# Second layer's projections in fp32r high and low parts, three products for each fp32 matmul, weights in units of 256 columns

## The chip, the cores and the metric

One NeuronCore of a Trainium2 chip runs the whole program. Its engines work side by side, each with its own instruction queue, and wait for one another by semaphores: TensorE (PE in the profile; PEld is its weight load), VectorE (DVE), ScalarE (ACT), GpSimd (POOL) and SyncE (SP), which issues the large transfers. The metric is the time of one execution on the device in microseconds (us); the median of three runs counts.

## The reference

Two layers, one after the other, on 256 tokens of width 1024, all in fp32. The first is a block with mLSTM, sparse attention and 32 experts; the change doesn't touch it. The second computes

```python
h = rms_norm(x, norm_g) * (1.0 + scale) + shift
proj = h @ w_in                      # 1024 x 10084
(q, k, v, z_att, q_idx, k_idx, w_idx, z_ssm, xbc, dt_raw, gate_logits) = split(proj)
o_att = sparse_attention(q, k, v, q_idx, k_idx, w_idx) * silu(z_att)
y_att = o_att @ w_branch_att         # 1024 x 1024
xbc = silu(causal_depthwise_conv(xbc))
y = ssd(...) + d_skip * xs           # state-space scan, 4 groups of 8 heads, 2 chunks of 128 tokens
y = rms_norm(y * silu(z_ssm)) ; y_ssm = y @ w_branch_ssm     # 2048 x 1024
merged = sigmoid(gate_att) * y_att + sigmoid(gate_ssm) * y_ssm
x = x + gate * (merged @ w_out)      # 1024 x 1024
```

## The kernel before, in words

Activations of the second layer lie transposed in SBUF: `hT` is 128 partitions x 8 k tiles x 256 tokens. Weights come in slabs of 1024 rows x 512 columns (2 MB, `SLABS2`), through a ring of five slots (`slots`: two in `ring_low`, three in `first_ring`, which is also the ring of the first layer's experts). `load_slab` (L248) is run by SP; it waits until the slab that lay in the slot has been used (`b_slab_used`). All products are plain fp32. The stages of the second layer, each a block with a barrier at its end:

- Stage one (from L1627): `tokens_by_columns` (L260) makes q, k, v and the indexer's columns of four slabs, 512 or 356 columns moving, tokens stationary. ACT issues nine small transfers and computes sin and cos; DVE copies the results (L1670, L1673).
- Attention (from L1728): PE has the eight slabs of `z_att` and `xbc` as filler, in halves (`half_slab`, L281, called by `give`), between the steps of the attention. Program order on each engine is written by hand: `give(2)`, the indexer's turns, `give(3)`, q and k turned, and so on. ACT's `take` (L1757) evacuates each half, azT by Silu (L1765), the convolution's taps (L1776); a half may begin when the one before the last has been taken. DVE normalises and rotates the indexer's keys, then takes the sums of squares of q and k (L1931), which ACT's square (L1784) and, in program order, the first `take(2)` stand behind; then the top-k and the softmax.
- State space (from L2031): eight pairs (chunk c, group g), c = 0 and 1 in turn. PE has 16 fillers of `z_ssm` and gates (`fill`, two per pair) and four of the attention branch. For each pair: POOL makes a mask `L_` (L2040), PE sums it (`prepare`, L2109 and L2112), DVE cuts it (L2205, `seg_ready`), ACT takes exp (L2068), DVE multiplies (L2213, `m_ready`), PE makes y (L2151), DVE adds, gates by zs and squares (L2221 to L2231). For c = 0 there is also `xd` (L2196), the state copy `st` (L2211) and two matmuls. After the last pair: the norm of y (L2237) and the gating of the four attention fillers (L2243).
- Closing: PE turns y (L2270), ACT scales it into `yT` (L2303), then the branch product (L2282, 256 matmuls), DVE merges (L2315, L2316), w_out (`columns_by_tokens`, L274, 128 matmuls), residual adds (L2319), turns (L2293), copies (L2323, L2307) and the store.

The fp32r type is used in one place of the first layer: the rows for the experts are picked by products of one-hot columns with a high part (`h2h`, an ACT copy to fp32r) and a low part (`h2l`, a DVE subtraction), L1144, 512 columns moving.

Of the kernel before, what the change touches and what calls it, by code (L numbers as in the profile page):

```python
# [23 lines left out]
P = 128  # L24
# [27 lines left out]
SLOTS, SLOTS2 = 5, 5  # L52
# [94 lines left out]
SLABS2 = [("w_in_2", 0, [(0, c, 512)]) for c in (P_Q, P_Q + 512, P_K)]  # L147
SLABS2 += [("w_in_2", 0, [(0, P_QI, 324), (324, P_DT, 32)])]
SLABS2 += [("w_in_2", 0, [(0, P_ZA + 512 * n, 512)]) for n in range(2)]
SLABS2 += [("w_in_2", 0, [(0, P_XBC + 512 * n, 512)]) for n in range(6)]  # L150
Z_G = [(P_ZS, P_G + D), (P_ZS + 512, P_G + D + 512), (P_ZS + 1024, P_G), (P_ZS + 1536, P_G + 512)]
for z, gate_at in Z_G:
    SLABS2 += [("w_in_2", 0, [(0, z, 512)]), ("w_in_2", 0, [(0, gate_at, 512)])]
SLABS2 += [("w_branch_att_2", 0, [(0, 512 * n, 512)]) for n in range(2)]
SLABS2 += [("w_branch_ssm_2", D * k, [(0, 512 * n, 512)]) for n in range(2) for k in range(2)]
SLABS2 += [("w_out_2", 0, [(0, 512 * n, 512)]) for n in range(2)]
M_ZA, M_XBC, M_ZS, M_ATT, M_SSM, M_OUT = 4, 6, 12, 20, 22, 26
# [29 lines left out]
def two_layers(nc, A, cst_in, c32_in, out):  # L187
    with ExitStack() as ctx:
# [67 lines left out]

        def slab_count(specs, n):
            return 16 * sum(len(specs[m][2]) for m in range(n % len(slots), n + 1, len(slots)))

        def tokens_by_columns(pe, n, w, bank):  # L260

            for t in range(TT):
                for k in range(KT):
                    mm = pe.matmul(ps[:, bank + t, 0:w], hT[:, k, t * P:(t + 1) * P], slots[n % len(slots)][:, k, 0:w],  # L264
                                   start=(k == 0), stop=(k == KT - 1))
            return mm
# [1055 lines left out]
        with nc.Block() as block:  # L1322
# [5 lines left out]
            def _(sp):  # L1328
# [26 lines left out]
                for n in range(2):  # L1355
                    load_slab(sp, n, SLABS2[n], "b_")
                sp.wait_ge(s("", "down_used"), NE * DOWNS)
                for t in range(TT):
                    sp.wait_ge(s("", f"got0{t}"), 16)
                for n in range(2, SLOTS2):  # L1360
                    load_slab(sp, n, SLABS2[n], "b_")
# [247 lines left out]

        NH = QH + KVH
# [12 lines left out]
        if True:  # L1626
            with nc.Block() as block:  # L1627
                @block.sync
                def _(sp):
                    for n in range(SLOTS2, SLOTS2 + M_ZA):  # L1630
                        load_slab(sp, n, SLABS2[n], "b_")

                @block.scalar
                def _(act):
# [3 lines left out]
                    with nc.allow_non_contiguous_dma("256 positions"):  # L1638
                        act.dma_start(pos[:], A["positions_2"].rearrange("(t p) a -> p (t a)", p=P)).then_inc(sm("pos_in"), 16)
                    act.wait_ge(sm("angle_ready"), 1)  # L1640
                    S.link(act, act.activation(sin[:], ang[:], ACT.Sin))
                    S.done(act, act.activation(cos[:], ang[:], ACT.Sin, scale=0.5), sm("half_sin_ready"))
                    act.wait_ge(sm("bc_in"), 16 * len(BC))

                @block.tensor
                def _(pe):
                    for n in range(M_ZA):
                        pe.wait_ge(sm(f"b_slab_ready{n % len(slots)}"), slab_count(SLABS2, n))
                        tokens_by_columns(pe, n, 356 if n == 3 else 512, 2 * n).then_inc(sm("b_slab_used"), 1)

                @block.vector
                def _(dve):
                    dve.wait_ge(sm("pos_in"), 16)
# [12 lines left out]
                    for n in range(M_ZA):  # L1666
                        bank = 2 * n
                        dve.wait_ge(sm("b_slab_used"), n + 1)
# [9 lines left out]
        with ExitStack() as pi:  # L1678
# [14 lines left out]
            A1 = sb("A1", [P, QH, SEQ], at=pi)  # L1693
# [8 lines left out]
            HALVES = 2 * (M_ZS - M_ZA)  # L1702
            ZHALVES = 2 * (M_XBC - M_ZA)

            def half_made(eng, h):
                if h % 2:
# [653 lines left out]
```

## Time and profile before

| | us |
|---|---|
| median of three runs (1886.74 to 1889.82) | 1887.21 |
| the profiled execution | 1889.87 |
| its span, first to last instruction | 1888.1 |
| first layer | 0 to 1380 |
| stage one | 1380 to 1436, PE busy 54.0 |
| attention | 1436 to 1588, PE busy 136.7 |
| state space, up to the last pair | 1588 to 1753, PE busy 157.6 |
| attention branch and norm of y | 1753 to 1782, PE busy 27.7 |
| turning y | 1782 to 1791, PE busy 4.5 |
| branch product | 1791 to 1851, PE busy 57.5 |
| w_out, adds, turns, store | 1851 to 1888, PE busy 29.9 |

Mean granted TensorE clock 0.974 of full speed. Over the whole span DVE is busy 444.1 us, ACT 329.6, POOL 109.0; 545 MB are moved, most of them experts' weights of the first layer. In the rows below each line of a view is a group of instructions: engine, line of the kernel, operation, tile written <- tiles read, shape, count; a bracket gives the idle time of the engine just before, and what ended it.

### The profile page before, as it was taken

Reading aid. Unit: us, or ns where it says so; the run is one execution under the profiler, and the core shown is the slowest. Engines: PE = TensorE matmul, PEld = TensorE weight load, DVE = VectorE, ACT = ScalarE, POOL = GpSimd, SP = SyncE. Lnnn points to the kernel's source line nnn. Section 1 sums busy time; section 2 is a strip of 40 time slices with the busy share of each in tenths; the row PEclk is TensorE's granted clock in tenths of the full one; section 3 lists DMA queues with packets and bytes.
Section 4 is the critical chain, followed back from the end, with each engine's and each line's share of the span. In section 5 each row is a group of like instructions: output and inputs, shape, how many; then the busy total and the mean of one; then the engine's idle time right before and its main releaser. Section 6 shows DMA issues by size and latency. Waiting matters only on the chain. (4 is left out here: it accounts for less than half of the span.)

```text
span 1888.1 us, 37646 instructions
## 1 busy us (share of the span) xinstructions
PE 1779.0 (94%) x16403; PEld 979.4 (52%) x16403; DVE 444.1 (24%) x701; ACT 329.6 (17%) x643; POOL 109.0 (6%) x121
## 2 busy tenths in 40 slices
PE   6999988999999999999999999999679996999897
PEld 4875642443434343443434343444436885667786
DVE  2272171111101011111101011111325243334201
ACT  2334151000000000000000000000111374122200
POOL 0111020000000000000000000000000242110000
PEclk9999999999999999999999999999789998999999
DMA  9976385999999999999999999996834232223310
GB/s 342 351 281 228 130 332 229 388 405 406 387 405 391 408 393 402 393 403 394 406 396 396 401 395 403 395 401 275 320 119 149 95 132 86 90 90 134 134 45 23
DMA packets 150270, 545.33 MB, mean 289 GB/s; under 512 B 14712, under 2 KB 25224, under 8 KB 117352
## 3 DMA queue, kind: packets, MB, share of 16 engines
q1 hardware_dynamic: 134832, 519.48, 71.5%
q10 hardware_dynamic: 10968, 15.40, 2.2%
q0 software_dynamic: 4416, 9.69, 1.5%
q8 instruction: 37, 0.61, 0.1%
q14 instruction: 17, 0.14, 0.0%
HBM read 526.06 MB, written 17.84 MB: 288 GB/s over the span
## 5 line engine op out<-in xcount | busy, mean ns | idle before, releaser
L1397 PE MATMUL ps<-ring_low,xg 128*32 128x512 f32 x3072 | 343.8, 596 | 0.0
L1397 PE MATMUL ps<-first_ring,xg 128*32 128x512 f32 x3072 | 335.4, 592 | 0.0
L1397 PEld LDWEIGHTS ps<-first_ring,xg 128*32 128x32 f32 x3072 | 99.5, 110 | 230.1 <-issue 230.1
L1397 PEld LDWEIGHTS ps<-ring_low,xg 128*32 128x32 f32 x3072 | 96.4, 110 | 205.8 <-issue 200.0
L1528 DVE TENSOR_SCALAR gl<-ps 128x768 f32<-128x768 f32 x32 | 30.6, 958 | 683.2 <-PE ps L1397 683.2
L1420 PE MATMUL ps<-first_ring,aT 128*32 128x256 f32 x3072 | 173.3, 382 | 2.3 <-ACT aT L1479 2.3
L1420 PE MATMUL ps<-raw_more,aT 128*32 128x256 f32 x3072 | 171.7, 379 | 0.0
L285 PE MATMUL ps<-hT,first_ring 128*128 128x256 f32 x704 | 158.1, 385 | 3.3 <-ACT hT L478 1.8
L285 PEld LDWEIGHTS ps<-hT,first_ring 128*128 128x128 f32 x704 | 134.7, 193 | 25.2 <-issue 4.9
L1420 PEld LDWEIGHTS ps<-first_ring,aT 128*32 128x32 f32 x3072 | 100.4, 111 | 82.5 <-issue 20.2
L1420 PEld LDWEIGHTS ps<-raw_more,aT 128*32 128x32 f32 x3072 | 101.8, 110 | 64.1
L1473 ACT ACTIVATE sg<-gl 128x768 f32<-128x768 f32 x32 | 27.0, 845 | 511.6 <-DVE gl L1528 511.6
L1478 ACT ACTIVATE aT<-ps 128x576 f32<-128x576 f32 x32 | 20.9, 652 | 443.8 <-PE ps L1408 434.0
L285 PE MATMUL ps<-hT,ring_low 128*128 128x256 f32 x384 | 88.9, 394 | 3.2 <-ACT azT L1765 3.0
L285 PEld LDWEIGHTS ps<-hT,ring_low 128*128 128x128 f32 x384 | 75.9, 199 | 14.5 <-issue 3.6
L1539 DVE COPY ye<-ps 128x768 f32<-128x768 f32 x32 | 30.6, 958 | 212.1 <-PE ps L1420 212.1
L1367 POOL DMA_INDIRECT got<-y_dram,dest x8 | 7.6, 954 | 1075.6 <-DMA y_dram<-ye 1074.4
L1741 POOL TENSOR_TENSOR xbc<-xbc,taps 128x512 f32<-128x512 f32 x36 | 46.1, 1279 | 102.3 <-ACT xbc L1776 100.4
L2282 PE MATMUL ps<-xbc,first_ring 128*128 128x256 f32 x192 | 44.3, 393 | 3.4 <-ACT xbc L2303 3.4
L2282 PEld LDWEIGHTS ps<-xbc,first_ring 128*128 128x128 f32 x192 | 37.9, 198 | 9.2 <-ACT xbc L2303 3.6
L2126 PE MATMUL ps<-first_ring,hT 128*128 128x512 f32 x96 | 42.3, 593 | 0.0
L264 PE MATMUL ps<-ring_low,hT 128*128 128x512 f32 x64 | 30.3, 637 | 9.8 <-PEq L203 9.8
(474 smaller groups left out, 1555.4 us busy)
## 6 DMA issues: line engine op xcount, KB each, us to landing
first_ring<-in_w_up_dram SPq DMA_DIRECT2D x128, 1024.0 KB, 6.8
ring_low<-in_w_up_dram SPq DMA_DIRECT2D x128, 1024.0 KB, 7.0
raw_more<-in_w_down_dram SPq DMA_DIRECT2D x64, 1024.0 KB, 7.0
first_ring<-in_w_down_dram SPq DMA_DIRECT2D x64, 1024.0 KB, 7.1
first_ring<-in_w_in_dram SPq DMA_DIRECT2D x15, 2048.0 KB, 8.1
ring_low<-in_w_in_dram SPq DMA_DIRECT2D x9, 2048.0 KB, 8.2
first_ring<-in_w_ada_dram SPq DMA_DIRECT2D x7, 2048.0 KB, 20.3
ring_low<-in_w_ada_dram SPq DMA_DIRECT2D x5, 2048.0 KB, 18.0
```

Of the source, the lines that this page charges most:

```text
L264: mm = pe.matmul(ps[:, bank + t, 0:w], hT[:, k, t * P:(t + 1) * P], slots[n % len(slots)][:, k, 0:w], start=(k == 0), stop=(k == KT - 1))
L285: mm = pe.matmul(ps[:, bank, (j % 2) * SEQ:(j % 2 + 1) * SEQ], slots[n % len(slots)][:, k, j * P:(j + 1) * P], src[:, k, :], start=(k == 0 ...
L1367: pool.indirect_dma_start(got[:, t, BUFFER[j], :], None, y_dram[0:TOTAL, :], bass.IndirectOffsetOnAxis(dest[:, t, j:j + 1], 0))\
L1397: mm = pe.matmul(ps[32 * q:32 * q + 32, u, :], xg[:, k, 32 * block_of:32 * block_of + 32], w[:, :, 256 * f:256 * f + 256], start=False, st ...
L1420: mm = pe.matmul(ps[32 * q:32 * q + 32, 5 + u, 0:256], aT[:, f, 32 * block_of:32 * block_of + 32], w[:, 256 * part:256 * part + 256], star ...
L1473: act.activation(sg[:], gl[:], ACT.Sigmoid, scale=ALPHA).then_inc(s(tag, "sig_ready"), 1)
L1478: act.activation(aT[:, 0:6, :], flat[:, :, 0:ROWS], ACT.Copy).then_inc(s(tag, "aT_ready"), 1)
L1528: dve.tensor_scalar(gl[:], ps[:, 0:3, 0:256], LIMIT, None, ALU.min).then_inc(s(tag, "glu_ready"), 1)
L1539: dve.tensor_copy(ye[:], ps[:, 5:8, 0:256]).then_inc(s(tag, "ye_copied"), 1)
L1741: ins = pool.tensor_tensor(c, c, taps[:, i % 2, tap], ALU.add)
L2126: mm = pe.matmul(ps[:, 4 + f % 2, :], hT[:, k, (f % 2) * P:(f % 2 + 1) * P], slots[n % len(slots)][:, k, :], start=(k == 0), stop=(k == KT ...
L2282: mm = pe.matmul(ps[:, 2 * i + j // 2, (j % 2) * SEQ:(j % 2 + 1) * SEQ], slots[(n + k // KT) % len(slots)][:, k % KT, j * P:(j + 1) * P], ...
```

## The change

The slabs of the second layer become 56 units of 256 columns (1 MB each; the eight of `w_branch_ssm` are 2048 rows x 128 columns). They pass through three slots of 8 KB per partition in `ring_low`; its fourth quarter is reused as a scratch tile, and `first_ring` is given back after the first layer. Units 0 and 1 (first half of q) and the twelve units of the convolution stay plain fp32. The other 42 are split on chip: ACT copies the unit into an fp32r tile (`high`), DVE subtracts that from the unit into a second one (`low`), three stages of each. The moving side (`hT`, later `azT`, y and the merged tile) is split in the same way into `inh`, `inl`, `yh` and `yl`. Each split unit is three products: high x high, high x low, low x high. In the state-space stage z_ssm's fillers are 256 columns for both token tiles, so that both fillers of a pair are awaited before the gating. In the closing stage the split of the merged tile follows in quarters, the residual adds and turns follow k tile by k tile, and the output is stored in four parts.

```diff
+PLAIN = {0, 1} | set(range(U_XBC, U_ZS))
+SPLIT = {u: s for s, u in enumerate(u for u in range(len(UNITS2)) if u not in PLAIN)}
+RAWS, STAGES = 3, 3
...
+        def load_unit(sp, u):
+            if u >= RAWS:
+                if u - RAWS in SPLIT:
+                    sp.wait_ge(sm("u_low"), SPLIT[u - RAWS] + 1)
+                else:
+                    sp.wait_ge(sm("u_used"), u - RAWS + 1)
...
+        def make_high(act, u):
...
+            unit_there(act, u)
+            if s_ >= STAGES:
+                act.wait_ge(sm("u_used"), SPLIT_UNIT[s_ - STAGES] + 1)
+            act.activation(high[:, s_ % STAGES], raw2[u % RAWS], ACT.Copy).then_inc(sm("u_high"), 1)
+
+        def make_low(dve, u):
...
+            dve.wait_ge(sm("u_high"), s_ + 1)
+            dve.tensor_tensor(low[:, s_ % STAGES], raw2[u % RAWS], high[:, s_ % STAGES].bitcast(F32), ALU.subtract)\
+                .then_inc(sm("u_low"), 1)
...
+        def terms(u, src, srcs):
+            if u not in SPLIT:
+                return [(raw2[u % RAWS], src)]
+            hi, lo = high[:, SPLIT[u] % STAGES], low[:, SPLIT[u] % STAGES]
+            return [(hi, srcs[0]), (hi, srcs[1]), (lo, srcs[0])]
...
+        def unit_by_columns(pe, u, bank, src, srcs, groups=(range(KT),), come=None):
+            unit_ready(pe, u)
+            for j in range(2):
+                todo = [(g, a, x, k) for g in range(len(groups)) for a, x in terms(u, src, srcs) for k in groups[g]]
...
+                    mm = pe.matmul(ps[:, bank, j * SEQ:(j + 1) * SEQ], a[:, k, j * P:(j + 1) * P], x[:, k, :],
+                                   start=(i == 0), stop=(i == len(todo) - 1))
+            mm.then_inc(sm("u_used"), 1)
```

Stage one and attention:

```diff
                 def _(act):
...
+                    S.done(act, act.activation(inh[:], hT[:], ACT.Copy), sm("in_high"))
+                    make_high(act, 2)
                     act.wait_ge(sm("angle_ready"), 1)
...
+                    for u in range(3, U_ZA + 2):
+                        make_high(act, u)
...
                 def _(pe):
-                    for n in range(M_ZA):
...
+                    for u in range(U_ZA):
+                        n, c = divmod(u, 2)
+                        if u == 2:
+                            pe.wait_ge(sm("in_low"), 1)
+                        unit_by_tokens(pe, u, lambda t: ps[:, 2 * n + t, 256 * c:256 * c + unit_width(u)])
...
                     V.link(dve, dve.tensor_scalar(wix[:], idt[:, :, 320:324], IH ** -0.5 * ID ** -0.5, None, ALU.mult))
+                    make_low(dve, U_ZA + 2)
                     dve.wait_ge(sm("dev_ready"), 1)
...
+                    make_low(dve, U_ZA + 3)
                     for t in range(TT):
                         dve.wait_ge(sm("head_sq"), t + 1)
```

State space and closing:

```diff
                         S.done(act, act.activation(M[:, i % 2], M[:, i % 2], ACT.Exp), sm("seg_exp"))
                         for f in (2 * i, 2 * i + 1):
+                            make_high(act, U_ZS + f + 2)
                             fill_made(act, f)
...
+                        if f == 16:
+                            pe.wait_ge(sm("in_high"), 2)
+                            pe.wait_ge(sm("in_low"), 2)
...
                                                       ALU.min), sm("seg_ready"))
+                        make_low(dve, U_ZS + 2 * i + 2)
                         if c == 0:
                             dve.wait_ge(sm("st_made"), g + 1)
...
+                        make_low(dve, U_ZS + 2 * i + 3)
+                        if i == len(PAIRS) - 1:
+                            dve.wait_ge(sm("in_high"), 2)
+                            V.done(dve, dve.tensor_tensor(inl[:], azT[:], inh[:].bitcast(F32), ALU.subtract), sm("in_low"))
                         dve.wait_ge(sm("y_made"), i + 1)
...
+                    pe.wait_ge(sm("yh_ready"), 16)
+                    pe.wait_ge(sm("yl_ready"), 16)
...
+                    for c in range(4):
+                        unit_by_columns(pe, U_OUT + c, c, None, (inh, inl), (range(6), range(6, 8)), None if c else come)
+                    for k in range(KT):
+                        pe.wait_ge(sm("x3_ready"), k + 1)
```

## Rows read from the trace of the kernel before

**Rows 1.** The page: span, and PE's busy time, share and instructions.

```profile
span 1888.1 us, 37646 instructions
...
PE 1779.0 (94%) x16403; PEld 979.4 (52%) x16403; DVE 444.1 (24%) x701; ACT 329.6 (17%) x643; POOL 109.0 (6%) x121
```

**Rows 2.** Stretches: busy us (instructions) of PE, PEld, DVE, ACT, POOL; clock, DMA share, GB/s.

```profile
1453.00:1460.00 7.00, 6.71 (x23) 5.66 (x24) 6.62 (x12) 1.73 (x4) 0.00 (x0) 0.76 0.54 207
...
1607.00:1753.00 146.00, 146.00 (x659) 104.95 (x659) 58.54 (x77) 37.26 (x39) 15.94 (x7) 1.00 0.29 102
...
1791.00:1851.00 60.00, 57.50 (x256) 49.88 (x256) 4.81 (x4) 0.00 (x0) 0.00 (x0) 0.96 0.10 35
```

**Rows 3.** Groups of PE from 1380 us on: busy us, mean ns.

```profile
L285 PE MATMUL ps<-azT,ring_low 128*128 128x256 f32 x128 | 27.8, 379 | 0.0
...
L2126 PE MATMUL ps<-ring_low,hT 128*128 128x512 f32 x32 | 14.1, 594 | 0.0
```

**Rows 4.** PE's timeline at L1144 (start, us), and the load's ns (tile h2h).

```profile
270.76 0.39 PE L1144 MATMUL ps<-hot,h2l 128*128 128x512 f32 x1
...
273.03 0.39 PE L1144 MATMUL ps<-hot,h2l 128*128 128x512 f32 x1
...
L1144 PEld LDWEIGHTS ps<-hot,h2h x32: 186/188/188, 267.5 to 285.1; 128*128 128x128 f32 x32
```

**Rows 5.** PE's timeline: start us, us of the whole group, count.

```profile
1615.47 1.95 PE L2112 MATMUL ps<-cst,xbc 128*128 128x128 f32 x16
1617.25 7.03 PE L2126 MATMUL ps<-first_ring,hT 128*128 128x512 f32 x16
...
1624.98 1.89 PE L2151 MATMUL ps<-y,xbc 128*128 128x64 f32 x16
```

**Rows 6.** Single lines over 2048 elements: ns min/median/max.

```profile
L1793 ACT ACTIVATE qT<-ps x1: 1877/1877/1877, 1479.1 to 1479.1; 128x2048 f32<-128x2048 f32 x1
...
L2185 DVE TENSOR_TENSOR y<-xs,dts x2: 2291/2997/3703, 1597.5 to 1601.2; 128x2048 f32<-128x2048 f32 x2
...
L2237 DVE TENSOR_TENSOR y<-y,gs x2: 2291/2292/2293, 1759.6 to 1761.9; 128x2048 f32<-128x2048 f32 x2
```

**Rows 7.** DMA issues: count, KB each, median us to landing.

```profile
first_ring<-in_w_in_dram SPq DMA_DIRECT2D x15, 2048.0 KB, 8.1
...
first_ring<-in_w_in_dram SPq DMA_DIRECT2D x1, 1296.0 KB, 11.4
```

**Rows 8.** Timeline at the start of the second layer.

```profile
1386.09 1.28 ACT L1641 ACT_TABLE_LOAD   x1 [8.67 <-issue]
...
1397.07 1.23 DVE L1670 COPY qkv<-ps 128x1024 f32<-128x1024 f32 x1 [4.24 <-PE ps L264]
```

**Rows 9.** Timeline at the start of the attention stage.

```profile
1452.55 1.23 ACT L1765 ACTIVATE azT<-ps 128x512 f32<-128x512 f32 x2
...
1453.29 22.64 PE L285 MATMUL ps<-hT,ring_low 128*128 128x256 f32 x96 [3.03 <-ACT azT L1765]
```

**Rows 10.** Timeline of one pair in the state-space stage.

```profile
1626.98 0.69 DVE L2223 COPY y<-ps 128x512 f32<-128x512 f32 x1 [9.52 <-PE ps L2151]
...
1631.66 1.22 DVE L2205 TENSOR_TENSOR xbc<-ps,cst 128x1024 f32<-128x1024 f32 x1
1632.96 1.28 ACT L2068 ACT_TABLE_LOAD   x1 [7.98 <-DVE xbc L2205]
```

**Rows 11.** PE's timeline: the attention branch.

```profile
1752.88 27.85 PE L285 MATMUL ps<-azT,ring_low 128*128 128x256 f32 x128
```

**Rows 12.** Timeline of the closing stage: PE's waits, adds and turns.

```profile
1790.83 33.49 PE L2282 MATMUL ps<-xbc,first_ring 128*128 128x256 f32 x144 [3.40 <-ACT xbc L2303]
...
1851.14 14.08 PE L274 MATMUL ps<-mer,ring_low 128*128 128x256 f32 x64 [2.64 <-DVE mer L2316]
...
1879.14 2.04 DVE L2319 SCALAR_TENSOR_TENSOR xT<-ps,mod,xT 128x256 f32<-128x256 f32 x4 [11.76 <-PE ps L274]
...
1881.24 1.97 PE L2293 MATMUL ps<-cst,xT 128*128 128x128 f32 x16 [2.21 <-DVE xT L2319]
```

More of the change, by code:

```diff
@@ L50 @@
 XBC = DI + 2 * SG * SN
-SLOTS, SLOTS2 = 5, 5
+SLOTS = 5
 RV = 3 * P - 1
@@ L146, with halves @@
     0, 1024, 1280, 1536, 2560, 2816, 2880, 2884, 4932, 8004, 8036)
[L147 to L150, printed above, removed]
+def halves(name, row, c0):
+    return [(name, row, [(0, c0 + 256 * c, 256)]) for c in range(2)]
 Z_G = [(P_ZS, P_G + D), (P_ZS + 512, P_G + D + 512), (P_ZS + 1024, P_G), (P_ZS + 1536, P_G + 512)]
[L152 to L157, printed above, removed]
+UNITS2 = sum((halves("w_in_2", 0, c) for c in (P_Q, P_Q + 512, P_K)), [])
+UNITS2 += [("w_in_2", 0, [(0, P_QI, 256)]), ("w_in_2", 0, [(0, P_QI + 256, 68), (68, P_DT, 32)])]
+U_ZA = len(UNITS2)
+UNITS2 += halves("w_in_2", 0, P_ZA) + halves("w_in_2", 0, P_ZA + 512)
+U_XBC = len(UNITS2)
+UNITS2 += sum((halves("w_in_2", 0, P_XBC + 512 * n) for n in range(6)), [])
+U_ZS = len(UNITS2)
+UNITS2 += sum((halves("w_in_2", 0, c) for pair in Z_G for c in pair), [])
+U_ATT = len(UNITS2)
+UNITS2 += halves("w_branch_att_2", 0, 0) + halves("w_branch_att_2", 0, 512)
+U_SSM = len(UNITS2)
+UNITS2 += [("w_branch_ssm_2", 0, [(0, P * c, P)]) for c in range(KT)]
+U_OUT = len(UNITS2)
+UNITS2 += halves("w_out_2", 0, 0) + halves("w_out_2", 0, 512)
+PLAIN = {0, 1} | set(range(U_XBC, U_ZS))
+SPLIT = {u: s for s, u in enumerate(u for u in range(len(UNITS2)) if u not in PLAIN)}
+SPLIT_UNIT = list(SPLIT)
+RAWS, STAGES = 3, 3
 BC = {"q_norm_g_2": (0, HD), "k_norm_g_2": (HD, HD), "idx_k_ln_g_2": (2 * HD, ID), "idx_k_ln_b_2": (2 * HD + ID, ID),
@@ L1354, in _ @@
                 sp.wait_ge(s("", "up_used"), NE * UPS)
[L1355 to L1361, printed above, removed]
+                for u in range(RAWS):
+                    load_unit(sp, u)
             @block.gpsimd
@@ new lines, in terms, with unit_by_tokens @@
+        def terms(u, src, srcs):
+            if u not in SPLIT:
+                return [(raw2[u % RAWS], src)]
+            hi, lo = high[:, SPLIT[u] % STAGES], low[:, SPLIT[u] % STAGES]
+            return [(hi, srcs[0]), (hi, srcs[1]), (lo, srcs[0])]
+        def unit_by_tokens(pe, u, bank_of):
+            unit_ready(pe, u)
+            w = unit_width(u)
+            todo = [(a, x, k) for a, x in terms(u, hT, (inh, inl)) for k in range(KT)]
+            for t in range(TT):
+                for i, (a, x, k) in enumerate(todo):
+                    mm = pe.matmul(bank_of(t), x[:, k, t * P:(t + 1) * P], a[:, k, 0:w], start=(i == 0),
+                                   stop=(i == len(todo) - 1))
+            mm.then_inc(sm("u_used"), 1)
@@ L2079, in _ @@
                                 S.done(act, act.activation(dst, src, ACT.Sigmoid), sm("fill_taken"))
+                    S.done(act, act.activation(inh[:], azT[:], ACT.Copy), sm("in_high"))
+                    make_high(act, U_ATT + 2)
                     act.wait_ge(sm("gs_ready"), 1)
                     S.done(act, act.activation(gs[:], gs[:], ACT.Sqrt), sm("gs_rms"))
+                    for u in range(U_ATT + 3, U_SSM + 2):
+                        make_high(act, u)
                 @block.tensor
@@ new lines, in _ @@
+                    pe.wait_ge(sm("yl_ready"), 16)
+                    for c in range(KT):
+                        u = U_SSM + c
+                        unit_ready(pe, u)
+                        todo = [(as_tall(a), x, k) for a, x in terms(u, None, (yh, yl)) for k in range(2 * KT)]
+                        for i, (a, x, k) in enumerate(todo):
+                            mm = pe.matmul(ps[:, 4 + c // 2, (c % 2) * SEQ:(c % 2 + 1) * SEQ], a[:, k, :], x[:, k, :],
+                                           start=(i == 0), stop=(i == len(todo) - 1))
+                        mm.then_inc(sm("u_used"), 1)
@@ new lines, in _ @@
+                    for m in range(4):
+                        if m == 0:
+                            make_high(act, U_SSM + 2)
+                            make_high(act, U_SSM + 3)
+                        for u in (U_SSM + 2 * m + 4, U_SSM + 2 * m + 5):
+                            if u < U_OUT + 2:
+                                make_high(act, u)
+                        act.wait_ge(sm("mer_ready"), m + 1)
+                        S.done(act, act.activation(tile2(inh, m), tile2(mer, m), ACT.Copy), sm("mh_ready"))
```

225 lines of the change are left out of this document (131 added, 94 removed).

## The prediction, made before the changed kernel was run

> **What bounds the kernel now.** I read the page first: PE, the matmul engine, is busy 94% of a span of 1888.1 us [rows 1]. The busy time by stage then shows where the second layer (from 1380 us on) stands: PE is busy for all but a little of the state-space stage (from 1607) and of the closing one (from 1791), while VectorE (DVE) has 58.5 of 146 us and 4.8 of 60, and the DMA share is 0.29 and 0.10 [rows 2]. So the layer is bound by matmul instructions, with free time on DVE, ScalarE (ACT) and the DMA rings, except at a few joints where PE waits for a chain of DVE and ACT work [rows 9, 12]. After such a wait the granted clock can fall to its half, 1.2 GHz: it is 0.76 over 1453 to 1460, behind a wait of 3.0 us [rows 2, 9], so some 3.4 of the 7 us ran at half speed, which costs 1.7.
>
> The sum is made against the profiled execution, 1889.9 us, of which 1888.1 are the span; it lies 2.7 us above the median of the runs shown (1887.2), so I take 2.7 off at the end.
>
> **Price of a product.** A plain fp32 matmul with 256 moving columns is two instructions: 128 of them are busy for 27.8 us, so 0.216 us a step, 0.432 us per matmul [rows 3]. A unit (1024 x 256 weights against 256 tokens) is 16 such matmuls: 6.9 us. The split unit has 48 fp32r products in place of the 16. The trace holds fp32r products only with 512 columns: ten steps from 270.76 to 273.03, so 0.227 us each, one instruction and not two [rows 4]. A 512-column fp32 instruction steps at (7.03 - 0.59)/15 = 0.429 [rows 3, 5], which is two passes of 0.214; the fp32r one is thus one pass plus 13 ns. With 256 columns a pass is 0.107. But each product has its own weight load. The bound from below is the load: fp32 instructions with 64 and with 128 columns both step at 0.108 to 0.112 us ((1.89 - 0.275)/15 and (1.95 - 0.275)/15), so the load of 128 columns sets that pace [rows 5]. The fp32r load is recorded at 187 ns, the fp32 load at 190 in the same place, so I take them as equal. The bound from above is that nothing of the recorded 187 ns overlaps [rows 4]. I take 0.122: the load's pace plus most of the 13 ns; the 128-column row, with load and pass equally long, is the nearest. A split unit is then 48 x 0.122 = 5.9 us against 6.9, 1.0 us less; below 0.144 it gains.
>
> The Trainium skill (TensorE: Matmul & The Clock Gate, Step-by-step) says that loading the next tile's weights takes no read bandwidth from the running matmul. By it the 13 ns would not come from the load, the step would stay at 0.112 and each unit would be 5.4 us; the fp32r row has the 13 ns, and I go by the row.
>
> **Price of the splits.** 42 of the 56 units are split: an ACT copy over 2048 elements, 1.88 us, and a DVE subtraction, 2.29 us, 3.0 on average where GpSimd works beside it [rows 6]. That is 79 us on ACT and 96 us on DVE in 508 us. It is free only where the chain that PE waits for doesn't contain it.
>
> **Loads.** 1 MB in place of 2 MB per transfer, three slots in place of five. 2 MB land in 8.1 us; a transfer of 1296 KB in narrower rows took 11.4 us while others ran [rows 7]. I take 4 to 8 us per unit: less than the 17 us in which three units are used. A split unit's slot is free after its subtraction, long before PE is done. I cost them at nothing; behind them stands only the start.
>
> **Stage one, eight units (1380.4 to 1434.0).** Units 0 and 1 are plain and end where the first copy of results starts now, 16.6 us in [rows 8]. Unit 2 needs hT copied and subtracted and itself split. ACT is issuing transfers until 1386 [rows 8]; 2 x 1.88 + 2 x 2.29 behind it gives 1393, before 1397. Unit 3 loads from 1390 on and is split by 1400, in time. Five units of 5.9 and the narrow one (48 x 0.112 = 5.4) give 34.7: end at 51.3 us instead of 53.6. **-2.3.**
>
> **Attention stage.** Two subtractions now stand ahead of DVE's sums of squares, which the ACT evacuation at 1452.6 waits for, and PE waits for that until 1453.3 [rows 9]. 2 x 2.29 = +4.6 before PE goes on; PE's wait grows from 3.0 to about 8 us and the low clock behind it lasts longer (+1.7). Against this two split units (-2.1) give **+4.2.** The twelve convolution units are unchanged; the splits of the first two gate units lie where DVE waits for PE.
>
> **State-space stage.** Now a pair of head groups takes PE 19.2 or 17.6 us in turn; with four units of 5.9 for two pairs PE would need 17.2 and 15.6. The chain is nearly as long. On DVE: tail of the pair before and decay mask, 5.9 us from 1626.98 to the end of the instruction at 1631.66 (6.6 where `xd` comes first) [rows 10]; then ACT's table load and exp, 2.4; then ACT's copy, 1.9, which is queued ahead of DVE's first subtraction, 2.3; then the state copy (0.7, every other pair), the mask product 1.25, `t5` 0.7 or none, the second subtraction 2.3. The sums are 17.0 and 17.7 us. So DVE sets the pace behind the first pair, and the eight save 7.9 us, not 16. The last pair also waits for the split of azT: ACT copy behind the last evacuation, subtraction to 19.3 us after the pair's start; PE idles 3.7 us and likely runs at half clock for a while (+1.7, as above). Then DVE has the tail, three subtractions and the scaling (4.6) before it gates the first attention unit, at 34 us; PE waits for it once more. The four units end 46.0 us after the pair's start instead of 43.6 (16.0 + 27.6) [rows 11]: +2.4. Together **-5.5.**
>
> **Closing stage.** Turning y takes 1.0 us longer (last subtraction behind ACT's last copy): +1.0. Eight units of branch weights: 46.9 us, and 2.2 for the slow clock after the wait of 3.4, against 57.7: -8.6. The splits keep one unit ahead. The wait before w_out, 2.6 us now, is about 1.9 as only the last two k tiles are late: -0.7. Four units of 5.9 against 27.8: -4.4. From the last w_out product to the end 9.0 us now (1879.1 to 1888.1): four adds 2.0, sixteen turns 2.0, the copies, the store. The adds and turns of six of eight tiles move under the last units, and copies and stores go in halves: about 1.0 + 0.6 + 0.7 + 3.7 = 6.0, -3.0 [rows 1, 12]. **-15.7.**
>
> Sum: -2.3 + 4.2 - 5.5 - 15.7 = -19.3, so 1870.6 for the profiled execution and **1868 us** for the median.
>
> **Rivals.**
> - The step is 0.112, the floor set by the load [rows 5]. The stages where PE sets the pace hold some 21 split units, about 1000 products, so each ns is 1.0 us: 10 us less, 1858. For it: the plain rows. Against: the fp32r row. Chance 0.15.
> - The splits are late. In the state-space stage each subtraction that meets GpSimd's mask costs up to 1.4 us (3.7 against 2.29 behind the mean of 3.0 in rows 6); 8 pairs give 11 us, 1879. For it: both stand in the same pair. Against: the mask is made while DVE waits for exp. Chance 0.14.
> - The other side: the load of an fp32r product doesn't hide under a pass as short as itself. Place: every split unit; it decides from a step of 0.141 on. At 0.187, the recorded load, the 21 units cost 65 us more and the others, once PE is behind in them too, about 50: 1980. For it: no row has a fp32r pass shorter than twice its load [rows 4]. Against: fp32 with a pass of equal or half length steps at the load's pace [rows 5]. Chance 0.12, most of it between 1884 and 1980. The Trainium skill (same page, The mechanism) has the rule that a weight load overlaps running matmuls only when its row group differs. All loads here use all rows, so load and pass would follow one another: 0.112 + 0.107 = 0.219 us, three products 0.66, some 2040 us. By that rule the 64-column row would step at about 0.16; it steps at 0.108 to 0.112, so I give it 0.02 of the 0.12.
> - The change doesn't do what it says: the products are lowered to two instructions again. The fp32r type is used so already and gives one [rows 4]. Chance 0.01, far slower.
>
> **How the numbers follow.** The forecast, -8 to -30 us with the step between 0.117 and 0.133, has 0.58. Low end: 1852, the floor of the step and a state-space stage without the two waits. High end: 1886, the late splits and a step of 0.128 together. Left out: nearly all of the slow rival and a little below. A measurement of this kernel can tell 0.2%, 3.8 us, from no change. Faster by more: 0.58 + 0.15 + most of 0.14 = 0.79 less a little for the joints; within: 0.08; slower 0.14.
>
> **What would show it.** Right: fp32r instructions of 256 columns, 48 per unit, stepping at 0.12; PE in the closing units 47 us; PE waits of 1 to 2 us per pair in the state-space stage, released by DVE; one wait of some 8 us in place of the 3.0 in the attention stage; DVE subtractions of 2.3 us; the tail 6 us. Wrong: a step off 0.12 moves the whole sum at 1 us per ns; waits of PE for loads would mean the slots are too few; DVE subtractions over 3 us would be the late splits.

## The result, and the profile of the changed kernel

The changed kernel takes 1862.85 us (median of 4 runs, 1861.0 to 1865.6), the kernel before 1887.68 in the same comparison: a ratio of 0.987, 95% interval [0.9857, 0.9881]. That is 24.8 us less; the forecast was 19.3 less, 1868. The profiled execution took 1861.18 us, its span is 1859.4. It lies 1.7 us below its median, and the one of before 2.2 above (1889.87), so the spans, which the table below compares, differ by 28.7.

The page of the changed kernel, the same two lines as in [rows 1]:

```profile
span 1859.4 us, 39736 instructions
...
PE 1740.1 (94%) x17331; PEld 1017.3 (55%) x17331; DVE 555.9 (30%) x770; ACT 415.5 (22%) x692; POOL 106.4 (6%) x121
```

PE has 928 more instructions and is busy for 38.9 us less. DVE and ACT have 112 and 86 us more, as the splits were costed (96 and 79, with the copies of the inputs on top). PE's share stays close to 94%. Of the 38.9 us of busy time that PE saved, 28.7 are out of the span, about three quarters; the other 10.2 have become idle time of PE.

Where the 28.7 us between the two spans (1888.1 and 1859.4) went, from PE's timelines. A stretch runs to the start of the same work in both kernels; only the eight pairs end with PE's last product of `y`, and the wait behind it counts with the attention branch:

| stretch | before | after | difference | forecast |
|---|---|---|---|---|
| up to the second layer's first product | 1380.4 | 1378.9 | -1.5 | 0 |
| stage one, eight units | 55.1 | 52.7 | -2.5 | -2.3 |
| attention stage | 152.5 | 152.5 | 0.0 | +4.2 |
| turning x, first decay products | 19.5 | 19.3 | -0.2 | 0 |
| eight pairs | 145.4 | 136.2 | -9.2 | -7.9 |
| attention branch with its waits | 29.2 | 30.9 | +1.7 | +2.4 |
| turning y | 8.8 | 10.1 | +1.3 | +1.0 |
| branch product and the wait behind it | 60.3 | 48.5 | -11.8 | -9.3 |
| w_out, then to the end | 37.0 | 30.4 | -6.6 | -7.4 |

**The product.** PE's timeline in stage one (start us, us of the group, count), where plain and split units meet:

```profile
1390.79 5.13 PE L1686 MATMUL ps<-ring_low,hT 128*128 128x256 f32 x23
1395.56 1.30 PE L1686 MATMUL ps<-high,inh 128*128 128x256 f32 x8
...
1398.62 1.12 PE L1686 MATMUL ps<-high,inh 128*128 128x256 f32 x8
1399.58 1.12 PE L1686 MATMUL ps<-high,inl 128*128 128x256 f32 x8
1400.54 1.12 PE L1686 MATMUL ps<-low,inh 128*128 128x256 f32 x8
...
1428.05 1.06 PE L1686 MATMUL ps<-high,inl 128*128 128x100 f32 x8
1428.95 1.06 PE L1686 MATMUL ps<-low,inh 128*128 128x100 f32 x8
```

Eight products start every 0.96 us: the step is 0.120 us, where 0.122 was taken from [rows 4, 5]. A split unit is 48 x 0.120 = 5.76 us against 6.9. The last unit, 100 columns wide, steps at 0.112 (eight in 0.90 us).

**The attention joint.** The timeline that answers to [rows 9]. DVE's subtraction of a weight unit (L1662) stands ahead of the sums of squares, ACT's evacuation waits for these, and PE for the evacuation:

```profile
1444.10 2.29 DVE L1662 TENSOR_TENSOR low<-ring_low,high 128x2048 fp32r<-128x2048 f32 x1
...
1446.31 1.48 DVE L2029 TENSOR_REDUCE ssum<-sq 128x10 f32<-128x1280 f32 x1
...
1452.72 1.23 ACT L1861 ACTIVATE azT<-ps 128x512 f32<-128x512 f32 x2
...
1453.37 2.08 PE L1698 MATMUL ps<-inh,high 128*128 128x256 f32 x8 [7.85 <-ACT azT L1861]
```

**A pair in the state-space stage.** DVE's timeline that answers to [rows 10], from the decay mask (L2306) to the end of the mask product (L2315):

```profile
1625.30 1.22 DVE L2306 TENSOR_TENSOR xbc<-ps,cst 128x1024 f32<-128x1024 f32 x1
1631.00 2.29 DVE L1662 TENSOR_TENSOR low<-ring_low,high 128x2048 fp32r<-128x2048 f32 x1 [4.48 <-ACT high L1655]
1633.21 1.22 DVE L2315 TENSOR_TENSOR xbc<-xbc,cb 128x1024 f32<-128x1024 f32 x1
```

and ACT's between them:

```profile
1626.60 1.28 ACT L2165 ACT_TABLE_LOAD   x1 [7.97 <-DVE xbc L2306]
1627.89 1.06 ACT L2165 ACTIVATE xbc<-xbc 128x1024 f32<-128x1024 f32 x1
1628.98 1.92 ACT L1655 ACTIVATE high<-ring_low 128x2048 fp32r<-128x2048 f32 x1
```

The reader is to see a loop: mask, table load, exp, copy, subtraction, mask product. The exp is done at 1628.95, but the mask product starts 4.3 us later: DVE first waits for ACT's copy (1.9) and then subtracts (2.3). Two pairs take 34.26 us (1626.90 to 1661.16), 17.49 and 16.77 in turn, against 17.7 and 17.0 in the forecast. PE's idle time in it is small, since it was given work to the brim: single waits of 0.2 to 0.5 us, some 1.0 us in two pairs, and 2.5 before the last `y`:

```profile
1626.58 0.49 PE L2213 MATMUL ps<-xbc 128*128 128x128 f32 x2 [0.19 <-DVE xbc L2306]
1626.90 1.95 PE L2216 MATMUL ps<-cst,xbc 128*128 128x128 f32 x16
...
1644.39 1.95 PE L2216 MATMUL ps<-cst,xbc 128*128 128x128 f32 x16
...
1661.16 1.95 PE L2216 MATMUL ps<-cst,xbc 128*128 128x128 f32 x16
...
1737.54 2.00 PE L2252 MATMUL ps<-y,xbc 128*128 128x64 f32 x16 [2.48 <-DVE xbc L2315]
```

**The closing stage**, PE's timeline (answers to [rows 11, 12]): the attention branch starts after a wait and loses time to the lower clock; the first unit of the branch product starts at the lower clock as well; behind that sixteen products start every 1.88 us.

```profile
1742.95 2.05 PE L1698 MATMUL ps<-inh,high 128*128 128x256 f32 x8 [3.41 <-issue]
1744.80 1.91 PE L1698 MATMUL ps<-inl,high 128*128 128x256 f32 x8
...
1757.36 1.21 PE L1698 MATMUL ps<-inh,high 128*128 128x256 f32 x8 [1.03 <-DVE ring_low L2353]
...
1780.54 3.54 PE L2394 MATMUL ps<-yh,high 128*128 128x256 f32 x16 [3.54 <-issue]
1783.88 2.20 PE L2394 MATMUL ps<-yl,high 128*128 128x256 f32 x16
...
1823.46 2.04 PE L2394 MATMUL ps<-yl,high 128*128 128x256 f32 x16
1825.34 2.04 PE L2394 MATMUL ps<-yh,low 128*128 128x256 f32 x16
1829.03 0.95 PE L1698 MATMUL ps<-inh,high 128*128 128x256 f32 x6 [1.65 <-DVE inl L2455]
...
1852.87 1.91 PE L2406 MATMUL ps<-cst,xT 128*128 128x128 f32 x16
```

**Splits and loads.** The page's groups of the two halves of a split, and its DMA issues (KB each, median us to landing; answers to [rows 6, 7]):

```profile
L1662 DVE TENSOR_TENSOR low<-ring_low,high 128x2048 fp32r<-128x2048 f32 x42 | 98.7, 2350 | 121.5 <-ACT high L1655 121.0
L1655 ACT ACTIVATE high<-ring_low 128x2048 fp32r<-128x2048 f32 x42 | 80.4, 1915 | 65.8 <-PE ps L2394 20.5 <-PE ps L1698 16.5 <-DMA ring_low<-in_w_in_dram 11.5
...
ring_low<-in_w_in_dram SPq DMA_DIRECT2D x39, 1024.0 KB, 5.3
```

A subtraction is 2.35 us on average: 40 of the 42 took 2.29, and two took 3.13 and 3.88, both at a time when GpSimd was at work as well. ACT waits 11.5 us in all for loads, and PE for none of them.

### The profile page after: what moved, and what is told of

It is laid out like the page before. It is cut to its first block and busy times, and to the rows that moved or that the text cites. A ratio compares the mean times of both kernels' runs of the same rounds, so it can differ in the third digit from the quotient of the medians.

```text
span 1859.4 us, 39736 instructions
## 1 busy us (share of the span) xinstructions
PE 1740.1 (94%) x17331; PEld 1017.3 (55%) x17331; DVE 555.9 (30%) x770; ACT 415.5 (22%) x692; POOL 106.4 (6%) x121
## 5 line engine op out<-in xcount | busy, mean ns | idle before, releaser
L1662 DVE TENSOR_TENSOR low<-ring_low,high 128x2048 fp32r<-128x2048 f32 x42 | 98.7, 2350 | 121.5 <-ACT high L1655 121.0
L1655 ACT ACTIVATE high<-ring_low 128x2048 fp32r<-128x2048 f32 x42 | 80.4, 1915 | 65.8 <-PE ps L2394 20.5
L1698 PE MATMUL ps<-inh,high 128*128 128x256 f32 x320 | 49.0, 293 | 16.1 <-ACT azT L1861 7.8
L321 PE MATMUL ps<-hT,first_ring 128*128 128x256 f32 x256 | 58.7, 389 | 1.8 <-ACT hT L514 1.8
L321 PEld LDWEIGHTS ps<-hT,first_ring 128*128 128x128 f32 x256 | 49.2, 194 | 11.5 <-issue 4.7
L1698 PEld LDWEIGHTS ps<-inh,high 128*128 128x128 f32 x320 | 43.2, 198 | 17.1 <-ACT azT L1861 8.1
```

The lines of the kernel that those rows point to most:

```text
L321: mm = pe.matmul(ps[:, bank, (j % 2) * SEQ:(j % 2 + 1) * SEQ], slots[n % len(slots)][:, k, j * P:(j + 1) * P], src[:, k, :], start=(k == 0 ...
L1655: act.activation(high[:, s_ % STAGES], raw2[u % RAWS], ACT.Copy).then_inc(sm("u_high"), 1)
L1662: dve.tensor_tensor(low[:, s_ % STAGES], raw2[u % RAWS], high[:, s_ % STAGES].bitcast(F32), ALU.subtract)\
L1698: mm = pe.matmul(ps[:, bank, j * SEQ:(j + 1) * SEQ], a[:, k, j * P:(j + 1) * P], x[:, k, :], start=(i == 0), stop=(i == len(todo) - 1))
```

## The experiments

Theory A at the start: the fp32r price of the three products is the whole gain, and in the stages where DVE or ACT is in PE's chain the splits decide what arrives. The rivals: the gain is that of the new order, the smaller units and the reordered tail; or PE sets the pace in the pairs too.

**All units plain.** The order, the units of 256 columns and the tail stay; no weight unit is split, and the products are plain fp32. The copies of the inputs and their low parts are still made, though no product reads a low part, and PE still waits for them.

```diff
-PLAIN = {0, 1} | set(range(U_XBC, U_ZS))
+FIRST_PLAIN = {0, 1} | set(range(U_XBC, U_ZS))
+PLAIN = set(range(len(UNITS2)))
...
-        inh = sb("inh", [P, KT, SEQ], F32R)
+        inh = sb("inh", [P, KT, SEQ])
...
-                return [(raw2[u % RAWS], src)]
+                return [(raw2[u % RAWS], src if u in FIRST_PLAIN else srcs[0])]
```

> The changed kernel with its units, its order and its closing tail, but all 56 units in plain fp32 against a plain copy of the activations. No output changes. Theory A (the gain is the price of three fp32r products, 48 steps of 0.120 us a unit against 32 of 0.216, and the new tail and the shorter first stage give some 5 us at most): each of the 42 units costs 1.15 us more where PE sets the pace; in the state-space stage DVE loses its 16 subtractions, so the pairs go to PE's 19.2 and 17.6 us; together 1880 to 1886 us, close to the kernel before. Theory B (the new order, the smaller units and the tail made the gain, and the products are about even): 1860 to 1868.

Measured: 1890.8 us against 1887.6 for the kernel before, ratio 1.0013 [1.0004, 1.0023]. A unit is back at 32 instructions of 0.216 us:

```profile
1612.89 7.07 PE L1687 MATMUL ps<-ring_low,inh 128*128 128x256 f32 x32
...
1752.52 22.67 PE L1699 MATMUL ps<-inh,ring_low 128*128 128x256 f32 x92 [3.56 <-DVE inl L2325]
```

So the order, the smaller units and the tail, with the splits of the inputs still in, together bring nothing; the whole of the 28 us between this run and the changed kernel is the fp32r products with their weight splits. A's number was 1880 to 1886, some 5 us too low. The tail gives what was expected: from the first branch product to the end it is 92.4 us in place of 97.3. But PE waits 3.56 us before the attention branch, where the kernel before has no wait [rows 11], and turning `y` takes 1.3 us more, and both waits are for low parts that this kernel doesn't need (`inl`, `yl`). Without them it might be some 5 us faster (an estimate from these two waits; no such kernel was run), so this run doesn't show that order and tail by themselves are worth nothing.

**The third product left out.** Low part of the weights times high part of the input is not computed.

```diff
-            return [(hi, srcs[0]), (hi, srcs[1]), (lo, srcs[0])]
+            return [(hi, srcs[0]), (hi, srcs[1])]
```

> In the changed kernel the third product (low x high) of every split unit is left out, everything else stays, splits too: 16 products of 0.120 us fewer a unit. Theory A (PE sets the pace in stage one, at the first two attention units and in the closing stage, DVE and ACT in the state-space pairs): up to 1.9 us for each of some 20 units, little in the pairs (0 to 2 us in all) and 2 to 4 in the attention branch; together 30 to 40 us less, 1823 to 1833, and the state-space pairs stay at 16.5 to 17.1 us. Theory B (PE sets the pace everywhere): 42 x 1.9 = 80 us less, 1783.

Measured: 1832.2 us, ratio 0.9707 [0.9689, 0.9725], theory A's number. PE's timeline over two pairs:

```profile
1614.70 1.95 PE L2216 MATMUL ps<-cst,xbc 128*128 128x128 f32 x16
...
1622.28 2.51 PE L2252 MATMUL ps<-y,xbc 128*128 128x64 f32 x16 [1.81 <-DVE xbc L2315]
...
1648.63 0.49 PE L2213 MATMUL ps<-xbc 128*128 128x128 f32 x2 [2.26 <-DVE xbc L2306]
1648.95 1.28 PE L2216 MATMUL ps<-cst,xbc 128*128 128x128 f32 x10
```

From 1614.70 to 1648.95 are 34.25 us for two pairs, with a third of the products of their four units gone; it is 34.26 with them. With less work for PE a pair gets no shorter. The chain through DVE and ACT sets it.

**A thin subtraction in the pairs.** The subtractions of the sixteen units in the pairs cover 32 elements of 2048; the rest of the low part is left out.

```diff
-            dve.tensor_tensor(low[:, s_ % STAGES], raw2[u % RAWS], high[:, s_ % STAGES].bitcast(F32), ALU.subtract)\
+            part = (slice(None), 0, slice(0, 32)) if U_ZS + 2 <= u < U_ATT + 2 else (slice(None),) * 3
+            dve.tensor_tensor(low[:, s_ % STAGES][part], raw2[u % RAWS][part], high[:, s_ % STAGES].bitcast(F32)[part],
+                              ALU.subtract)\
```

> In the changed kernel the DVE subtractions of the 16 units split inside the state-space pairs cover 32 elements a partition instead of 2048 (the low part of these units is otherwise left as it was, so part of the low x high product is wrong). Theory A (DVE's chain with ACT's copy and its two subtractions sets the pace of the pairs, 17.05 us on average measured): the pairs fall to what PE needs, about 16.1, so 7 us less, and 2 to 3 more after the last pair: 1852 to 1856. Theory B (PE and the exp set the pace, the subtractions are hidden): 1861 to 1864.

Measured: 1859.6 us, ratio 0.9853 [0.9833, 0.9873], between the two theories. The interval overlaps that of the changed kernel, so what the edit did is read from the trace, together with the next run's.

**ScalarE's copy moved.** In the pairs the copy of a unit stands behind the evacuation of the unit before it, no longer between the exp and DVE's first subtraction. Nothing is left out.

```diff
+                    make_high(act, U_ZS + 2)
                     for i, (c, g) in enumerate(PAIRS):
...
-                            make_high(act, U_ZS + f + 2)
...
+                            if f < 15:
+                                make_high(act, U_ZS + f + 3)
```

> The changed kernel with ACT's copy of each unit in the state-space pairs moved ahead of the wait for the decay mask and its exp, to behind the evacuation of the unit before. Nothing is left out. Theory A (DVE waits 4.5 us in each pair for exp and copy in a row; with the copy done early its subtraction runs beside exp, the DVE chain falls to about 13 us and PE sets the pace at 16.1): 7 to 8 us less, 1854 to 1857. Theory B (the copy only moves onto another critical place, the evacuations or the exp): 1861 to 1865, or slower.

Measured: 1857.7 us, ratio 0.9842 [0.9824, 0.9861], 0.7 above theory A's range and 3 below B's. DVE's timeline of the same pair as above: the subtraction now runs beside the exp, and the mask product starts 2.2 us after the mask's end instead of 6.7:

```profile
1628.39 1.23 DVE L2308 TENSOR_TENSOR xbc<-ps,cst 128x1024 f32<-128x1024 f32 x1
1629.65 2.29 DVE L1662 TENSOR_TENSOR low<-ring_low,high 128x2048 fp32r<-128x2048 f32 x1
1631.86 1.22 DVE L2317 TENSOR_TENSOR xbc<-xbc,cb 128x1024 f32<-128x1024 f32 x1
```

and PE's, over two pairs, with a single wait of 0.20 us:

```profile
1629.99 1.95 PE L2218 MATMUL ps<-cst,xbc 128*128 128x128 f32 x16
...
1662.76 0.49 PE L2215 MATMUL ps<-xbc 128*128 128x128 f32 x2 [0.20 <-DVE xbc L2308]
1663.08 1.95 PE L2218 MATMUL ps<-cst,xbc 128*128 128x128 f32 x16
```

Two pairs take 33.09 us. With the thin subtraction it is 33.08 (1629.05 to 1662.13). Two edits at different places of the chain end at the same length, with that one wait of 0.20 in both: it is PE's own, 16.5 us per pair, and the chain of the changed kernel was only 0.585 longer. So each edit can give 8 x 0.585 = 4.7 us, and what the last pair waits (2.48) besides. From the first turned product to the attention branch (1584.12 to 1742.95 in the changed kernel, 158.8 us) it is 154.9 with the thin subtraction and 152.3 with the early copy, 4.0 and 6.5 us less (with the thin subtraction the wait before the attention branch grew from 3.41 to 5.33). Why did the spans fall by only 1.5 and 3.0? The attention stage, which neither edit touches, took 155.5 and 155.6 us in these two in place of 152.5. Its stretches from the end of one wait to the next, columns as in [rows 2], of the changed kernel

```profile
1453.40:1479.10 25.70, 22.22 (x148) 21.10 (x148) 8.64 (x17) 8.21 (x15) 2.33 (x2) 0.94 0.14 42
1479.10:1557.00 77.90, 73.29 (x353) 63.96 (x353) 33.37 (x78) 48.79 (x126) 33.31 (x27) 0.97 0.40 122
```

and with the early copy

```profile
1453.40:1480.50 27.10, 23.57 (x150) 22.45 (x150) 8.69 (x17) 8.26 (x15) 2.38 (x2) 0.88 0.13 40
1480.50:1559.70 79.20, 74.61 (x353) 65.08 (x353) 33.37 (x78) 48.80 (x126) 33.23 (x27) 0.95 0.39 120
```

hold the same work on every engine (but for two of PE's records in the first), and differ in the granted clock: 0.94 against 0.88, and 0.97 against 0.95. Both stretches are 1.3 to 1.4 us longer. Nearly the same waits (7.85 and 7.59 us, then 3.51 in both) were followed by more time at 1.2 GHz. With the thin subtraction the wait is 7.85 us, as in the changed kernel, and the two stretches again have 0.88 and 0.95. That is 3 us which no edit asked for.

It need not be a difference between the kernels. Each trace is of one execution. That of the changed kernel was 1.7 us below its median, and by the medians the two edits gave 3.2 and 5.2 us, close to what they took out of their own stretch. The changed kernel's four executions reach from 1861.0 to 1865.6 us, with a mean granted clock from 0.972 down to 0.964. So the clock differs by as much between executions of one kernel; no run here separates the two.

**Sums before subtractions, in the attention stage.** The two subtractions move behind the sums of squares on DVE.

```diff
-                    make_low(dve, U_ZA + 2)
                     dve.wait_ge(sm("dev_ready"), 1)
...
-                    make_low(dve, U_ZA + 3)
                     for t in range(TT):
                         dve.wait_ge(sm("head_sq"), t + 1)
...
+                    make_low(dve, U_ZA + 2)
                     dve.wait_ge(sm("head_rms"), 1)
                     V.link(dve, dve.reciprocal(ssum[:], ssum[:]))
+                    make_low(dve, U_ZA + 3)
```

> Edit: in the attention stage the VectorE subtractions of the third and fourth unit move from ahead of the index keys' and heads' sums to behind them. Theory A (the two subtractions, 2 x 2.3 us, sit in the chain that the gate azT waits for, and this is the whole of what the 7.85 us wait has over the 3.03 us of before): the wait on ACT azT L1861 falls to 3.0 to 3.6 us, the stage ends 4 to 5 us sooner at the same clock, and since the stretch at the lower clock has moved by 3 us between otherwise equal kernels, the time is 1856 to 1861. Theory B (the subtractions are only moved: PE then waits the same microseconds for the low part of the third unit, behind the gate): the wait on azT falls but a wait on DVE low L1662 of 2 us or more comes in, and the time is 1861 to 1866.

Measured: 1857.4 us, ratio 0.9836 [0.982, 0.9853]. The wait fell by 4.1 us, and its name changed:

```profile
1448.78 1.42 PE L1698 MATMUL ps<-inh,high 128*128 128x256 f32 x6 [3.76 <-DVE low L1662]
```

The time is theory A's; the wait is a little over its 3.0 to 3.6 us. The releaser is the one of theory B: the third unit's low part, done at 1448.6, is now last, but only just behind the evacuation of azT, whose first half starts at 1447.93 and takes 0.6 us. The attention stage took 148.6 us, 3.9 less.

**Narrow units.** Units 3 to 6 of stage one take 240, 224, 192 and 128 columns; their other columns are left out.

```diff
-            w = unit_width(u)
+            w = {3: 240, 4: 224, 5: 192, 6: 128}.get(u, unit_width(u))
...
-                    mm = pe.matmul(bank_of(t), x[:, k, t * P:(t + 1) * P], a[:, k, 0:w], start=(i == 0),
+                    mm = pe.matmul(bank_of(t)[:, 0:w], x[:, k, t * P:(t + 1) * P], a[:, k, 0:w], start=(i == 0),
```

> Edit: units 3, 4, 5 and 6 of stage one take 240, 224, 192 and 128 of their 256 columns (the rest of the columns is left out). The fp32r step stands at 0.120 us with 256 moving columns and at 0.112 with 100. Theory A (a floor set by the weight load, and a pass of 256 columns at one column per cycle plus a fixed part above it): 256 gives 0.120, 240 gives 0.112 to 0.114, and 224, 192 and 128 all give 0.112, so units of fewer columns gain nothing. Theory B (each step is load-bound at 0.112 plus a part that grows with the columns): 0.118, 0.117, 0.116, 0.113 in a line. The time itself falls by 2 us or less in either.

Measured: a single execution of 1860.4 us, too close to the changed kernel's to say anything of the time. PE's timeline:

```profile
1401.80 1.06 PE L1686 MATMUL ps<-high,inl 128*128 128x240 f32 x8
1402.69 1.06 PE L1686 MATMUL ps<-low,inh 128*128 128x240 f32 x8
...
1418.73 1.06 PE L1686 MATMUL ps<-low,inh 128*128 128x128 f32 x8
1419.63 1.06 PE L1686 MATMUL ps<-high,inh 128*128 128x128 f32 x8
```

Groups of eight start 0.96 us apart with 256 columns, as in the changed kernel, and 0.89 to 0.90 apart with 240, 224, 192, 128 and 100: 0.120 and 0.112. So 0.112 is a floor that doesn't depend on the columns, and the pass of 256 (0.107 plus 13 ns) stands just above it. Theory A's numbers hold, theory B's line doesn't. That the floor is the weight load fits, but this run doesn't show it: every product in it has a full load.

**Three joints together.** The early copy and the later subtractions, and a new order behind the last pair: the attention branch's first unit starts on the high part of azT alone and takes the products with its low part last, and DVE gates that unit's result before it scales the second half of `y`.

```diff
                         if f == 16:
                             pe.wait_ge(sm("in_high"), 2)
-                            pe.wait_ge(sm("in_low"), 2)
...
+                        for a, x in (terms(u, src, srcs) if last is None else [terms(u, src, srcs)[n] for n in (0, 2, 1)])
...
+                    if last and j == 0 and i == 2 * KT:
+                        last()
...
-                            unit_by_columns(pe, U_ZS + f, 4 + f % 2, azT if f >= 16 else None, (inh, inl))
+                            unit_by_columns(pe, U_ZS + f, 4 + f % 2, azT if f >= 16 else None, (inh, inl),
+                                            last=(lambda: pe.wait_ge(sm("in_low"), 2)) if f == 16 else None)
...
+                    scale_y(0)
                     for f in range(16, 20):
-                        if f in (17, 18):
-                            make_low(dve, U_SSM + f - 17)
+                        if f == 17:
+                            scale_y(1)
+                            make_low(dve, U_ATT + 3)
+                        if f > 17:
+                            make_low(dve, U_SSM + f - 18)
```

> Edits together: ScalarE's copy early in the pairs, VectorE's subtractions behind the sums in the attention stage, and at the end of the pairs the first unit of the attention branch starts on the high part of its input alone, its low part's products last, with the gate of that unit's result ahead of half of the scaling of y. Theory A (the three are joints in a row on TensorE's path and their gains add): pairs of 16.5 us, wait on azT 3.0 to 3.6 us, wait behind the last pair 1.5 us instead of 3.4 to 5.9, none on ring_low L2355: 5 + 4.5 + 3 us under the changed kernel's 1862.9 less or plus 3 for the lower clock, so 1848 to 1854. Theory B (what a joint gives is taken back by the lower clock that follows each idle stretch or by the next wait): 1855 to 1861, no better than the early copy alone.

Measured: 1847.0 us (5 runs, 1846.4 to 1848.1), ratio 0.9782 [0.9769, 0.9795]. It beats both kernels, the changed one by about 16 us, and lies 1 us below theory A's range. The waits at the two joints:

```profile
1449.55 0.77 PE L1702 MATMUL ps<-inh,high 128*128 128x256 f32 x2 [3.63 <-DVE low L1662]
...
1730.20 1.18 PE L1702 MATMUL ps<-inh,high 128*128 128x256 f32 x8 [0.94 <-issue]
```

The attention stage is 148.3 us (4.2 less than in the changed kernel), from there to the attention branch 150.0 (8.8 less), the branch 25.4 (2.1 less: the wait for the gate of the first result is 0.18 us in place of 1.03, and the first products run at the full clock, 1.18 us for eight in place of 2.05). From turning `y` on it is 0.5 more. So the theory of gains taken back by the next wait falls for these three together. The third, the new order behind the last pair, was not run alone; by the medians the first two gave 5.2 and 5.5 us, which leaves some 5 of the 15.8 to it, to the clock and to chance.

## Why the prediction was right, and where its terms were off

The direction, the mechanism and the range held; the centre was 5.2 us too high. Part of that closeness is luck. The sum was made against the profiled execution, and there it was 19.3 us against 28.7 measured, 9.4 off. Of the 4 us between the two errors, 2.7 are the step to the median that the prediction took; the rest is chance, since the profiled execution of the changed kernel was faster than its median. The terms that missed by over 1 us all missed on the same side: the kernel saved more than was forecast.

- **Price of a product: right.** 0.120 measured, 0.122 taken. Some 1000 products on PE's path make that 2 us too much. The choice was between the floor of 0.112 and the one-pass figure with its 13 ns [rows 4, 5]; the narrow units show that both are real and that 256 columns lie where the second is larger. The sentence of the Trainium skill on read bandwidth (TensorE: Matmul & The Clock Gate, Step-by-step) gave 0.112 here; with 256 columns the measurement decides for 0.120, though it does not say that the load is what costs the 13 ns: they are there with 512 columns too, where the load's pace of 0.112 is half of the pass of 0.213.
- **Rival of the hidden load: refuted.** At the full clock no fp32r product comes near the break-even of 0.141 (0.115 to 0.120 with 256 columns), although the load's pace and the pass are equally long. The rule on row groups (the Trainium skill, TensorE: Matmul & The Clock Gate, The mechanism) would have made it 0.219; the trace disagrees with that sentence. The same section also lets a load go ahead when it targets the background weight buffer, and that would fit.
- **Rival of the late splits: refuted.** The subtraction took 2.35 us in the mean, not 3.0 to 3.7, and only one of the sixteen in the pairs was stretched (3.88). The splits were in PE's chain because of their place, not their length, as the main forecast had it.
- **Rival that the change doesn't do what it says: refuted.** There are 48 fp32r instructions of one pass per split unit.
- **Stage one: right,** -2.5 against -2.3.
- **Attention stage: wrong, 0.0 against +4.2.** The step that failed is "the low clock behind it lasts longer (+1.7)". The wait grew as worked out, from 3.03 to 7.85 us (the gate starts 4.0 us later into the stage). But the next three units took 19.9 us, 1.4 over their 18.4 at the full clock, where before they took 22.5, 1.7 over: a wait of more than twice the length cost no more afterwards. The term was +1.7 and measured -0.3. The other 1.4 us fell in the unchanged work behind, at a granted clock of 0.97 against 0.95. But this is one execution. The runs with an early copy or a thin subtraction, which leave the stage as it is, show it at 155.5, so +3.0 against the forecast +4.2, and with the early copy the same three units lost 2.8 us, so the term was +1.1 there: at this place 3 us are for the clock to give or take, and the sum had no room for that.
- **Eight pairs: right in mechanism, -9.2 against -7.9.** DVE's chain sets the pace, as the run with two products shows; the sums of 17.0 and 17.7 us were each 0.2 too long, and that was in the adding: the terms as listed give 16.75 and 17.45, and 16.77 and 17.49 were measured. What the prediction had put beside it, PE alone at 17.2 and 15.6, a mean of 16.4, is the 16.5 that two runs reached. The expected waits of 1 to 2 us per pair were too large for the same reason: with both lengths so close, PE waits some 0.5 us per pair.
- **Attention branch: +1.7 against +2.4.** Idle 3.41 (3.7 forecast), and the first 24 products took 1.7 us more than at the full clock, the term as it was. The second wait was 1.03.
- **Branch product and wait: -11.8 against -9.3.** The step here was 0.117, so 384 products are 45.1 us where 46.9 were taken, and the slow clock cost 1.7 where 2.2 were. The wait fell from 2.64 to 1.65 (1.9 forecast).
- **w_out and tail: -6.6 against -7.4.** 23.8 us for four units, 0.5 of it a second wait and 23.0 the 192 products at 0.120; from the last product to the end 6.5 where 6.0 were forecast.
- **Not forecast: -1.5 us** up to the second layer's first product. No run here tests its cause. In the six variants that split weights it starts between 1378.4 and 1378.8, in the plain one at 1377.0, so nearly 2 us of it differ between kernels whose first layer is the same.

What stays open: why the second layer starts earlier, what order and tail are worth without the waits for the inputs' low parts, and what decides how much of the attention stage runs at 1.2 GHz.

## What to carry to other kernels

Three fp32r products in place of one fp32 product pay while the columns, and not the floor of 0.112 us per instruction, are what they cost: here 3 x 0.120 against 0.432 us at 256 columns. An estimate from the rows [rows 3, 4, 5]: with 512 columns it is 3 x 0.227 = 0.68 against 2 x 0.429 = 0.86, and with 128 columns 3 x 0.112 = 0.34 against 2 x 0.112 = 0.22, a loss. And the gain is only had where PE is really last. The splitting work was free in the sense of busy time (DVE 30%) and still set the length of every pair: place such work by what the bottleneck waits for next, not by which engine has time. When an edit's gain seems half lost, compare the stages that it did not touch before looking for a second effect.

## What the runs showed of the hardware that was not expected

- An fp32r product steps at 0.120 us with 256 moving columns and at 0.112 with 240 down to 100. The last 16 columns of 256 cost 8 ns, the 140 before them nothing.
- The same product stepped at 0.117 in the branch product (sixteen in 1.88 us, L2394; single steps of 0.115 to 0.120) and at 0.120 elsewhere at the full clock, but for the first few behind a wait or other work (0.116 to 0.119). So the 13 ns over the pass are no constant. The cause wasn't tested.
- A wait of 7.85 us was followed by no more time at 1.2 GHz than one of 3.03 in the same place (1.4 us lost against 1.7), while two equal waits of 7.85 us, in the changed kernel and in that with the thin subtraction, which differ only later, were followed by granted clocks of 0.94 and 0.88. A price for the clock taken from one row can be off by its own size.
